# A two-model kernel on one core: norms split by columns and by halves of tokens, and modulations moved into the merge loop

## What is computed

```python
# first model, one block (its token mixers are left out)
x = x + gt1 * y                                   # y ends in merged @ w_out
hx2 = modulate(rms_norm(x, norm2_g[l]), sh2, sc2)
x = x + gt2 * conv_ffn(hx2, rows, w_up[l], ffn_conv_w[l], ffn_conv_b[l], w_down[l])
x = rms_norm(x, final_g)

# second model, two layers
hx = _rmsnorm(x, norm_g) * (1.0 + scale_x) + shift_x
hc = _rmsnorm(ctx, norm_g) * (1.0 + scale_c) + shift_c
px, pc = hx @ w_in, hc @ w_in                     # keys, values, queries, gates
...                                               # neighbourhood attention and grouped attention
x = x + gate_x * (merged @ w_out)
ctx = ctx + gate_c * (merged_c @ w_out)           # first layer only
```

## Time and profile before

| | us |
|---|---|
| median of three runs | 2992.94 (2992.8 to 2994.6) |
| the profiled execution | 2993.36 |
| its span in the trace | 2991.7 |

### The profile page before, as it was taken

How to read it: one execution, slowest core, us unless ns; L and a number is a source line. 1 busy time by engine, 2 the same in 40 slices (tenths; PEclk the granted TensorE clock), 3 DMA queues, 4 the chain that set the end, 5 groups by cost and what they waited for, 6 DMA issues and landing times.

```text
span 2991.7 us, 41281 instructions
## 1 busy us (share of the span) xinstructions
PE 2904.7 (97%) x16802; PEld 1686.2 (56%) x16802; DVE 1041.1 (35%) x2032; ACT 720.0 (24%) x1389; POOL 232.8 (8%) x296
## 2 busy tenths in 40 slices
PE   6899999999999999999998999999999899999998
PEld 2777777776444444444444567765555544775443
DVE  3455555553231234444312226521011312552011
ACT  3344444442200002212002226620000012462000
POOL 0222222220000000000000101000000001100000
PEclk9999999999999999999999999999999999999999
DMA  5111111103244433444321210001111122101222
GB/s 204 54 40 40 35 41 35 35 30 128 77 141 139 136 97 126 161 147 155 98 84 58 74 43 30 1 29 56 50 49 49 49 63 75 43 2 57 77 76 72
DMA packets 61301, 220.93 MB, mean 74 GB/s; under 512 B 6688, under 2 KB 8864, under 8 KB 60896
## 3 DMA queue, kind: packets, MB, share of 16 engines
q1 hardware_dynamic: 42512, 153.11, 16.2%
q0 software_dynamic: 14656, 56.93, 5.9%
q10 hardware_dynamic: 3984, 8.71, 0.8%
HBM read 215.01 MB, written 2.15 MB: 73 GB/s over the span
## 4 chain that ended last, share of the span: by engine, by line
PE 95%; DMA 1%; DVE 1%; ACT 1%; issue 1%; POOL 0%; DVEq 0%; ACTq 0%; POOLq 0%; SPq 0%
PE psum L366 92%; PE psum L735 3%; DMA arena<-in_ctxT 1%; DMA arena<-in_stream 0%; DMA arena<-in_mods 0%; PE psum L552 0%; DVE arena L1258 0%; ACT arena L923 0%; ACT arena L1043 0%; PE psum L505 0%; ACT arena L1146 0%; ACT arena L916 0%; DVE arena L1636 0%; ACT arena L910 0%; DVE arena L1650 0%
## 5 line engine op out<-in xcount | busy, mean ns | idle before, releaser
L366 PE MATMUL psum<-arena 64*64 64x64 f32 (+6 forms) x16002 | 2810.6, 359 | 74.2 <-ACT arena L923 15.7
L366 PEld LDWEIGHTS psum<-arena 128*128 128x128 f32 (+4 forms) x16002 | 1599.9, 161 | 1266.5 <-issue 1114.5
L1477 DVE SCALAR_TENSOR_TENSOR arena<-arena 128x1024 f32<-128x1024 f32 x128 | 149.2, 1220 | 5.1 <-DMA arena<-in_mods 4.8
L1730 DVE SCALAR_TENSOR_TENSOR arena<-arena,psum 128x512 f32<-128x512 f32 x32 | 21.2, 684 | 371.7 <-PE psum L366 371.7
L1146 ACT ACTIVATE arena<-psum,arena 128x512 f32<-128x512 f32 (+2 forms) x160 | 115.3, 728 | 31.2 <-DVE arena L1642 18.2
L1200 ACT ACTIVATE arena<-psum 128x512 f32<-128x512 f32 x32 | 19.1, 597 | 372.5 <-PE psum L366 372.5
L1604 DVE COPY arena<-psum 128x512 f32<-128x512 f32 x26 | 18.0, 692 | 238.8 <-PE psum L366 238.8
L735 PE MATMUL psum<-arena 128*128 128x128 f32 x704 | 94.2, 279 | 4.2 <-ACT arena L1146 4.0
L1821 POOL DMA_DIRECT2D arena<-in_bias x16 | 8.8, 552 | 1111.6 <-DVE arena L1614 849.6
L735 PEld LDWEIGHTS psum<-arena 128*128 128x128 f32 x704 | 76.3, 140 | 29.0 <-issue 14.8
L1815 POOL DMA_DIRECT2D arena<-in_mods x76 | 40.1, 528 | 670.0 <-DVE arena L1477 670.0
(11 more groups left out here) (206 smaller groups left out, 1340.5 us busy)
## 6 DMA issues: line engine op xcount, KB each, us to landing
arena<-in_stream SPq DMA_DIRECT2D x288, 512.0 KB, 3.6
arena<-in_mods POOLq DMA_DIRECT2D x80, 512.0 KB, 3.6
arena<-gc_rows POOLq DMA_DIRECT2D x16, 384.0 KB, 4.7
arena<-in_bias POOLq DMA_DIRECT2D x16, 384.0 KB, 3.9
arena<-in_xT ACTq DMA_DIRECT2D x1, 2048.0 KB, 18.2
out<-arena SPq DMA_DIRECT2D x1, 2048.0 KB, 7.2
arena<-in_conds ACTq DMA_DIRECT2D x1, 1536.0 KB
arena<-arena POOLq DMA_DIRECT2D x4, 384.0 KB, 4.3
```

The lines of the kernel that those rows point to most:

```text
L366: return pe.matmul(out, lhsT, rhs, start=start, stop=stop, skip_group_check=True)
L1477: m = stt(mjunk[:, b % 2, :] if x < len(conds) - 1 else slot, slot, 0.5, cb[:, c, :], ALU.mult, ALU.mult, accum_out=dst(x))
```

## The change

1. **Merge.** The eight gate blocks no longer stand ahead of the loop; each merge step now has four modulation blocks. Both bias additions come behind the loop.
2. **B.** Seven output tiles stay whole. The last one is computed as tokens 0 to 255 (into bank 7) and then 256 to 511 (into bank 2). Each half has its own update, square, sum, root, scale and shift. The first two up tiles run together, first on the first half of the tokens, then on the second.
3. **C.** Context's sum, root, scale and shift of the second model's first norm come in the middle of the down product. The value product makes all k for the two context chunks first, with the latent sum after the third k, and then all k for the four latent chunks. The banks are renumbered accordingly (`value_bank`).
4. **D.** The fourth and the last wide output tile are computed context first. Context's norm follows at once, the latent sum comes as in C.
5. The two-pass loops around these places are written out, and semaphore counts are renumbered (`ROOTS`, `NORMED`).

```diff
-SUMS = {0: KT + 1, 1: 2 * KT + 2, 2: 3 * KT + 4, 4: 4 * KT + 5}
+SUMS = {0: KT + 1, 1: 2 * KT + 2, 2: 3 * KT + 5, 4: 4 * KT + 6}
+ROOTS = {n: at + 1 for at, n in enumerate((0, "1a", "1b", "2c", 2, 3, "4c", 4))}
+NORMED = {n: KT * at for at, n in enumerate((0, "1a", "1b", "2c", 2, "4c", 4))}
...
+            def ctx_norm_sum(count):
+
+                pe.wait_ge(s("sqsum"), count)
+                mm(psum[:, 1, 0:CTX], ones, sqb[:, 1, SEQ:TOK]).then_inc(s("nsum"), 1)
...
+            def half_sum(h):
+
+                pe.wait_ge(s("sqsum"), SUMS[1] + h)
+                mm(psum[:, 4 + h, 0:CTX], ones, sqb[:, 1, halves[h]]).then_inc(s("nsum"), 1)
+
+            for j in range(KT):
+                pe.wait_ge(s("xo"), j - 3 + 4)
+                if j < KT - 1:
+                    product(T_OUT + j, MG, 4 + j % 4, None, ready=None if j else ("mg", FREE))
+                    continue
+                w = weights(pe, T_OUT + j)
+                for k in range(KT):
+                    m = mm(psum[:, 7, halves[0]], w[:, k * P:(k + 1) * P], MG[:, k, halves[0]], k == 0, k == KT - 1)
+                m.then_inc(s("out_part"), 1)
+                for k in range(KT):
+                    m = mm(psum[:, 2, halves[1]], w[:, k * P:(k + 1) * P], MG[:, k, halves[1]], k == 0, k == KT - 1)
+                    if k == 4:
+                        half_sum(0)
+                m.then_inc(s("used"), 1)
+
+            for h in range(2):
+                for k in range(KT):
+                    pe.wait_ge(s("H"), NORMED[("1a", "1b")[h]] + k + 1)
+                    for b in range(2):
+                        wk = weights(pe, T_UP + b)[:, k * P:(k + 1) * P]
+                        m = mm(psum[:, b, halves[h]], wk, H[:, k, halves[h]], k == 0, k == KT - 1)
+                        if h and k == KT - 1:
+                            m.then_inc(s("used"), 1)
+                    if not h and k == 2:
+                        half_sum(1)
...
+                for k in range(KT):
+                    near_values(k, range(XC, CH), NORMED["4c" if l else "2c"])
+                    if k == 2:
+                        pe.wait_ge(s("sqsum"), SUMS[4] + 1 if l else SUMS[2])
+                        mm(psum[:, 0, :], ones, sqb[:, 1, 0:SEQ]).then_inc(s("nsum"), 1)
+                for k in range(KT):
+                    near_values(k, range(XC), NORMED[4 if l else 2])
...
-            norm_root(1, (0, 1), False)
-            norm_shift(KT, ((0, SEQ, 0),), modT[:, 24:32, :])
+            norm_root("1a", ((0, CTX, 4),))
+            norm_shift(NORMED["1a"], ((0, CTX, 0),), modT[:, 24:32, :], range(3))
+            norm_root("1b", ((CTX, SEQ, 5),))
+            norm_shift(NORMED["1a"], ((0, CTX, 0),), modT[:, 24:32, :], range(3, KT))
+            norm_shift(NORMED["1b"], ((CTX, SEQ, 0),), modT[:, 24:32, :])
...
-            with dve.Fori(0, 2) as i:
-                for j in range(4):
-                    mod_block(B_GATE1 + j, lambda x: modf[:, bass.ds(8 * i + 2 * (16 + j) + x, 1)], ((0, 0),), i, 4)
-            add_bias(B_NORM2, modT, "b_mod", 16, 8, 1)
...
-                    for b in range(3):
-                        mod_block(B_NORM2 + 3 * j + b,
-                                  lambda x: modf[:, bass.ds(24 * i + 2 * (24 + 3 * j + b) + x, 1)], ((0, 0),), i, 12)
+                    for b in range(4):
+                        mod_block(B_GATE1 + 4 * j + b,
+                                  lambda x: modf[:, bass.ds(32 * i + 2 * (16 + 4 * j + b) + x, 1)], ((0, 0),), i, 16)
...
+            dve.wait_ge(s("out_part"), 1)
+            last_half(0)
+            norm_scale("1a", ((0, CTX, 0),), range(3))
+            dve.wait_ge(s("used"), T_OUT + KT)
+            last_half(1)
+            norm_scale("1a", ((0, CTX, 0),), range(3, KT))
+            norm_scale("1b", ((CTX, SEQ, 0),))
...
+                if i == 0:
+                    dve.wait_ge(s("gmod"), 4)
+                    norm_scale("2c", ((SEQ, TOK, 1),))
...
+                    dve.wait_ge(s("out_part"), 3)
+                    add_out(KT - 1, 1)
+                    last_squares(1, SEQ, TOK)
+                    norm_scale("4c", ((SEQ, TOK, 1),))
+                    dve.wait_ge(s("used"), T0 + L_OUT + KT)
+                    add_out(KT - 1, 0)
+                    last_squares(2, 0, SEQ)
```

More of the change, by code:

```diff
@@ L331, in decays, with value_bank @@
             return flat(decay[:, 2 * (i % 2):2 * (i % 2) + 2, :])
+        def value_bank(c):
+            return 4 + c if c < XC else 2 + c - XC
         def slot2(j):
@@ L674, in _ @@
                 product(T_MERGE + 3, U, 2, None, i, 4)
-            with pe.Fori(0, 2) as i:
-                for j in range(4):
[L677 to L681, removed]
+            halves = slice(0, CTX), slice(CTX, SEQ)
+            def half_sum(h):
+                pe.wait_ge(s("sqsum"), SUMS[1] + h)
+                mm(psum[:, 4 + h, 0:CTX], ones, sqb[:, 1, halves[h]]).then_inc(s("nsum"), 1)
@@ L682, in _ @@
+            pe.wait_ge(s("G"), 2)
+            product(T_UP + 2, H, 2)
+            product(T_UP + 3, H, 3)
+            with pe.Fori(1, FT // 2) as i:
                 for j in range(2):
                     pe.wait_ge(s("G"), 2 * i + j - 1 + 2)
-                    product(T_UP + 2 * j, H, 2 * j, None, i, 4, ready=None if j else ("H", KT))
+                    product(T_UP + 2 * j, H, 2 * j, None, i, 4)
                     product(T_UP + 2 * j + 1, H, 2 * j + 1, None, i, 4)
             pe.wait_ge(s("G"), FT + 2)
-            with pe.Fori(0, 2) as i:
+            for i in range(2):
@@ L905, in _, with norm_root, norm_shift @@
             f = act.activation
-            def norm_root(n, banks, wide, eps=vec("eps"), ctx_eps=vec("eps"), to=rnorm):
+            def norm_root(n, parts, eps=vec("eps"), to=rnorm):
                 act.preload_act_table_set("natural_log_exp_and_others")
[L909 to L912, removed]
+                act.wait_ge(s("nsum"), ROOTS[n])
+                for a, b, bank in parts:
+                    m = f(to[:, a:b], psum[:, bank, 0:b - a], ACT.Ln, bias=eps, scale=1.0 / D)
                 m.then_inc(s("nln"), 1)
[L914 to L920, removed]
+                act.wait_ge(s("nln"), ROOTS[n])
+                a = parts[0][0]
+                f(to[:, a:b], to[:, a:b], ACT.Exp, scale=-0.5).then_inc(s("rnorm"), 1)
+            def norm_shift(h0, parts, shift, ks=range(KT)):
+                for k in ks:
                     act.wait_ge(s("Hs"), h0 + k + 1)
@@ L1248, in squares_twice, with norm_scale @@
                 tt(plain_sum, plain_sum, x2, ALU.add).then_inc(s("sq"), 1)
-            def norm_scale(n, parts):
-                dve.wait_ge(s("rnorm"), n + 1)
-                for k in range(KT):
+            def norm_scale(n, parts, ks=range(KT)):
+                dve.wait_ge(s("rnorm"), ROOTS[n])
+                for k in ks:
                     for (a, b, j) in parts:
                         h, x, r = H[:, k, a:b], X[:, k, a:b], rnorm[:, a:b]
-                        if n >= 2 and not a:
+                        if n in (2, 4):
                             h = h.rearrange("p (c r) -> p c r", r=ROWS)
@@ L1676, in _ @@
                 L = f"{l}"
[L1677 to L1683 removed]
+                norm_scale(4 if l else 2, ((0, SEQ, 0),))
                 dve.wait_ge(s("b2load"), 32)
```

139 lines of the change are left out of this document (81 added, 58 removed).

## The result

The changed kernel takes 2955.6 us (median of four runs, 2954.1 to 2957.3) against 2992.9 (2992.3 to 2994.6) for the kernel before: a ratio of 0.9875 with a 95% interval of 0.9857 to 0.9892. Run twice more on other chips it took 2955.4 and 2955.2 beside 2991.7 and 2991.6. The forecast was 2957.5 with a range of 2954 to 2964, so 1.9 us too slow and inside the range. The profiled execution took 2954.9, a span of 2953.2; the one before had 2991.7.

The account below looks back on a forecast made before the run. TensorE (PE), busy 97% of the span, bounds the kernel; time is won only at its idle gaps and slow-clock stretches. Savings of 6.6 + 5.5 + 10.7 + 13.0 = 35.8 us gave about 2957.5 us, range 2954 to 2964.

Parts of the forecast that it names:

- B: End of the mixer's output and first up tiles: halves leave waits of 0.9 and 1.6 us, saving 5.5 us.
- C: Norm before the second model's first layer: context first cuts 53.3 us to 42.2 plus 0.4, saving 10.7 us.
- D: Norm before the second model's second layer: context first cuts 55.6 us to 42.2 plus 0.4, saving 13.0 us.
- A: Start of the merge loop: PE's 3.98 us wait and a slow stretch costing 2.6 us go, saving 6.6 us.
- Rival (1): Clock drops at the halved output and up tiles: 1.7 to 2.1 us less gain, 2959.5 us; 27%.
- rival (2): Second model's norms: value tile late or wait between passes, some 2 us each, 2961.5 us; 8%.
- Loops, nothing: Two-pass loops on PE and DVE become straight code: no gain taken, as no PE wait lies at a turn.
- The sum, 35.8: The four places' savings added, 6.6 + 5.5 + 10.7 + 13.0 = 35.8 us.
- (3): Narrow matmuls in the halved tiles and second layer's norm expose weight loads: 18 us, 2975.5 us; 4%.
- (4): Removed idles shift what follows and the slow stretch after the 1.97 us gap disappears: 2955.9 us; 5%.
- (5): PE waits for instructions in the 32 unrolled tiles: 1.3 us each, 41.6 us lost if all, 2999 us; 3%.
- (6): In-order DVE or ACT prevents the halves' overlap; only 4.0 us idle at the merge loop is won: 2989.4 us; 3%.

Follow-up runs that it names:

- A and B alone: Kernel before with the merge loop's change and the last output tile and first two up tiles in halves, second model's norms as before: 2981.8 us, ratio 0.9961.
- the merge alone: Kernel before with the modulation blocks moved into the merge loop and nothing else: 2988.37 us, ratio 0.9984.
- both kernels with loops written out: Kernel before with two-pass loops written out, no work moved: on PE and DVE 2990.88 us (ratio 0.9990), on DVE only 2990.48 us (ratio 0.9995).

## Why the prediction was right, point by point

**What bounds the kernel.** Right. Only PE's gaps and slow stretches moved; DVE and ACT do slightly more work than before, and it costs nothing.

**A, 6.6.** Measured 6.9: 3.98 of waiting and 2.6 of slow clock, and the blocks in the loop hidden. The 0.3 over it was not traced to a cause.

**B, 5.5.** Measured 5.3 where only A and B were changed; the whole change has 12.5 - 6.9 - 0.3 = 5.3 too. The waits came out 0.78 for 0.9 and 1.41 for 1.6. With T at 1098.80 (the end of the tile ahead, as in the trace before) they ended at T + 8.1 and T + 12.8, each 0.1 early, and the up pair was done at T + 24.3, 0.1 late: 29.67 - 24.34 = 5.3 once more. Rival (1), a quarter of the chance, did not happen.

**C, 10.7.** Measured 10.9. The value product took 42.1 us for the 42.2 of the sum. The four value tiles held through both passes cost nothing, so rival (2) is out at C and at D.

**D, 13.0.** Measured 13.4 from one copy on ACT to the other, with a layer of attention in between that differs by some tenths on its own; the value product is 42.1. The idle time in it was understood. That the size fits to 0.4 is in part no test, at C and at D: forecast and measurement count against the same trace of the kernel before, with its slow stretches. In four other traces with D as before (the merge alone, A and B alone, and both kernels with loops written out) the work behind D's first wait takes 182.8 us in place of 184.5. Against the kernel with A and B alone, C gains 12.6 and D 11.6, 24.2 in sum where the table has 24.3. So for either place some 1.7 us are a matter of which slow stretch a trace happened to have.

**Loops, nothing.** The reason given (no PE wait lies at a turn of a PE loop) held and was not enough: the loops' price was on DVE, between a wait and the operation behind it. On the old order that is 0.3 to 0.65 us at each of A, B, C and D, 1.8 in sum; the slow stretches behind them did not get shorter by it (D's did, but without it as well). It hardly mattered, since the change takes PE off those waits; the term that the forecast missed is the 0.3 at the first down tile.

**The sum, 35.8.** Counted from the tanh 37.0: 6.9 at A, 5.3 at B and 0.3 at the down tile (the table's 12.5), then 10.9, 13.4 and 0.3. The 1.5 in front of the tanh can't be put to the change: over the 14 traces that event lies between 841.8 and 847.1, in those of the changed kernel between 842.3 and 842.7, in the others with its merge loop between 841.8 and 844.5 (and the 847.1), in those with the old one between 842.9 and 845.2. So of the 2.7 us by which the trace gains more than 35.8, 1.5 lie in a part of the kernel that scatters by more than that, and 1.2 in the places counted.

**The other rivals.** (3), exposed weight loads: 0.216 us from one narrow record to the next, so none. The Trainium skill ("TensorE: Matmul & The Clock Gate", LDWEIGHTS) puts a load at columns / 1.2 GHz, which makes 107 ns for 128 columns; in B's last stretch PEld has 53 loads in 9.78 us, 0.18 each in the records, beside 52 narrow matmul records, and PE is busy for all of the 11.17 us, so the loads are hidden behind the stream here. The measurement decides against the estimate of 14 us. (4), the slow stretch at layer 1 disappears: not in the three traces of the changed kernel, though it can. (5), waits for instructions: 1.5 to 2.3 us in all in those traces, none in the written-out tiles. (6), halves held back: no.

## What to carry to other kernels

A norm between two products costs PE its whole chain of sum, root, scale and shift; work that doesn't depend on all tokens, put between the last product and the sum, hides it, and both the idle time and the slow stretch behind it are won. Price such a step by the order of events on each engine, not by busy shares, and count the clock with it: here 12 of 38 us were clock. What one trace shows of a slow stretch is good to some 1.7 us. On the engine that hands over, look at the sequencer's lines between wait and operation too, since here the time between them was on the path wherever PE waited for it, and went with the loop.

## What the runs showed of the hardware

In this kernel a PE wait of about 2 us was on the edge of dropping its clock. 1.41 in B didn't in five traces, 1.93 didn't in two, 2.45 did in one, 1.96 at layer 1 did in 12 of 14, 2.02 at layer 2 in 2 of 14, and the same program had it both ways. Each drop made the next 5 us run at 0.66 to 0.68 in the mean and cost 1.6 to 1.7. So one profile's slow stretch behind such a wait is a chance, not a price, and two kernels compared by one trace each can differ by it. Behind longer waits too: with 3.63 and 4.85 at D in three kernels, the work from the first of them to the attention took 184.46 us in one trace and 182.81 and 182.82 in the two others.

Inside a loop over an index DVE took 0.25 us from PE's last matmul to its first operation and 0.11 from that to the next; in straight code 0.03 and 0.02 (output tiles, kernel before and DVE's loops written out).
